# Two heavy down chunks of each pair multiplied as plain float32, and gathered rows copied out by ScalarE alone

## What is computed

```
def swiglu(h, wg, wu, wd):
    return (jax.nn.silu(h @ wg) * (h @ wu)) @ wd

def moe_swiglu(h, w_router, wg, wu, wd):
    ...
    logits = (xt @ w_router).astype(jnp.float32)
    top_v, top_i = lax.top_k(logits, TOP_K)          # TOP_K = 2
    gates = jax.nn.softmax(top_v, axis=-1)
    gate = jnp.sum(jax.nn.one_hot(top_i, N_EXPERTS, dtype=jnp.float32) * gates[..., None], axis=1)
    y = jnp.zeros_like(xt)
    for e in range(N_EXPERTS):
        y = y + gate[:, e:e + 1].astype(xt.dtype) * swiglu(xt, wg[e], wu[e], wd[e])
```

## Time and profile before

| | |
|---|---|
| median of 3 runs | 1589.66 us (1588.79 to 1591.21) |
| the profiled execution | 1587.91 us; span of its instructions 1586.1 us |
| mean granted TensorE clock | 0.986 of full |
| TensorE busy | 1518.3 us, 96% of the span |
| VectorE busy | 1293.6 us, 82% |
| ScalarE busy | 1091.3 us, 69% |
| mixture of experts | from 668 us to the end, 4 pairs |
| DMA | 462.70 MB, 1 MiB for each chunk |

### The profile page before, as it was taken

The page is one execution under the profiler, slowest core; times in us unless marked ns, Lnnn a source line. Parts: engine busy times, 40 slices in busy tenths (PEclk is TensorE's granted clock), DMA queues, the critical chain, the costliest instruction groups (busy, mean ns, idle before and its releaser), DMA issues.

```text
span 1586.1 us, 20833 instructions
## 1 busy us (share of the span) xinstructions
PE 1518.3 (96%) x7379; PEld 1259.1 (79%) x7379; DVE 1293.6 (82%) x1595; ACT 1091.3 (69%) x1435; POOL 117.6 (7%) x242
## 2 busy tenths in 40 slices
PE   6999999999999999699999999999899999999995
PEld 5788788888888888588887788788788787788784
DVE  5686585566545556789999999999999999999998
ACT  3664564645434364278888788888788878788876
POOL 3333431101000010100000000000000000000000
PEclk9999999999999999699999999999999999999998
DMA  9645444535546554369999999999999999999995
GB/s 328 202 157 172 156 158 136 182 115 186 173 146 201 195 179 159 131 240 373 391 398 406 390 378 387 386 407 403 379 387 387 391 409 400 375 387 386 398 409 226
DMA packets 203364, 462.70 MB, mean 292 GB/s; under 512 B 7934, under 2 KB 12428, under 8 KB 203132
## 3 DMA queue, kind: packets, MB, share of 16 engines
q1 hardware_dynamic: 200304, 453.80, 78.3%
q0 software_dynamic: 1904, 5.38, 1.3%
q10 hardware_dynamic: 1052, 2.19, 0.4%
HBM read 460.29 MB, written 1.05 MB: 291 GB/s over the span
## 4 chain that ended last, share of the span: by engine, by line
PE 73%; DVE 11%; DMA 9%; issue 2%; DVEq 2%; ACT 2%; SPq 0%; ACTq 0%
PE ps L2149 8%; PE ps L2151 8%; PE ps L2150 8%; PE ps L2605 7%; PE ps L2607 7%; PE ps L2606 7%; PE ps L2620 6%; DVE wlo_sb L1373 6%; PE ps L2621 6%; DMA raw_sb<-moe_wu 6%; PE ps L2658 2%; DMA raw_sb<-w_in 2%; ACT whi_sb L998 2%; PE ps L2567 1%; DMA raw_sb<-moe_wg 1%
## 5 line engine op out<-in xcount | busy, mean ns | idle before, releaser
L1373 DVE TENSOR_TENSOR wlo_sb<-raw_sb,whi_sb 128x1024 fp32r<-128x1024 f32 x662 | 771.9, 1218 | 37.3 <-ACT whi_sb L998 34.7
L998 ACT ACTIVATE whi_sb<-raw_sb 128x1024 fp32r<-128x1024 f32 x662 | 657.1, 1051 | 153.1 <-PE ps L2607 97.8
L1365 DVE TENSOR_TENSOR wlo_sb<-raw_sb,whi_sb 128x1024 fp32r<-128x1024 f32 (+2 forms) x198 | 230.2, 1204 | 145.6 <-ACT whi_sb L990 144.6
L990 ACT ACTIVATE whi_sb<-raw_sb 128x1024 fp32r<-128x1024 f32 (+2 forms) x198 | 192.3, 1022 | 163.5 <-PE ps L2151 132.1
L2149 PE MATMUL ps<-whi_sb,xlo_sb 128*128 128x512 f32 (+2 forms) x544 | 213.0, 392 | 3.8 <-DVE xlo_sb L1412 3.8
L2151 PE MATMUL ps<-whi_sb,xhi_sb 128*128 128x512 f32 (+2 forms) x544 | 208.7, 384 | 0.0
L2150 PE MATMUL ps<-wlo_sb,xhi_sb 128*128 128x512 f32 (+2 forms) x544 | 208.7, 384 | 0.0
L2605 PE MATMUL ps<-whi_sb,xlo_sb 128*128 128x512 f32 x448 | 181.2, 405 | 4.5 <-DVE wlo_sb L1373 3.8
L2607 PE MATMUL ps<-whi_sb,xhi_sb 128*128 128x512 f32 x448 | 175.4, 392 | 0.0
L2620 PE MATMUL ps<-whi_sb,xhi_sb 128*128 128x512 f32 x448 | 175.1, 391 | 0.0
L2621 PE MATMUL ps<-wlo_sb,xhi_sb 128*128 128x512 f32 x448 | 174.6, 390 | 0.0
(11 more groups left out here) (394 smaller groups left out, 2127.0 us busy)
## 6 DMA issues: line engine op xcount, KB each, us to landing
raw_sb<-moe_wg SPq DMA_DIRECT2D x113, 1024.0 KB, 9.9
raw_sb<-moe_wd SPq DMA_DIRECT2D x112, 1024.0 KB, 10.5
raw_sb<-moe_wu SPq DMA_DIRECT2D x109, 1024.0 KB, 10.6
raw_sb<-w_in SPq DMA_DIRECT2D x40, 1024.0 KB, 5.1
raw_sb<-w_out SPq DMA_DIRECT2D x16, 1024.0 KB, 5.1
raw_sb<-ffn_wg SPq DMA_DIRECT2D x10, 1024.0 KB, 5.1
raw_sb<-ffn_wu SPq DMA_DIRECT2D x10, 1024.0 KB, 5.2
raw_sb<-ffn_wd SPq DMA_DIRECT2D x10, 1024.0 KB, 5.0
```

Of the source, the lines that this page charges most:

```text
L990: nc.scalar.activation(whi[i % SPLIT][:, c:c + k // 2, 0:n], raw[i % RAW][:, c:c + k // 2, 0:n], ACT.Copy).then_inc(hi_ready, 1)
L998: nc.scalar.activation(whi[i % SPLIT][:, c:c + KC // 2, :], moe_raw(i, l)[:, c:c + KC // 2, :], ACT.Copy).then_inc(hi_ready, 1)
L1365: op = V.tensor_tensor(wlo[i % SPLIT][:, c:c + k // 2, 0:n], raw[i % RAW][:, c:c + k // 2, 0:n], whi[i % SPLIT][:, c:c + k // 2, 0:n], ALU ...
L1373: op = V.tensor_tensor(wlo[i % SPLIT][:, c:c + KC // 2, :], moe_raw(i, l)[:, c:c + KC // 2, :], whi[i % SPLIT][:, c:c + KC // 2, :], ALU.s ...
```

## The change

Chunks for which `whole(step)` holds (places 62 and 64 of a pair, 52 and 54 of the first) are no longer split. TensorE multiplies them as plain float32, straight from the raw buffer, with unsplit activations of block 2 in `act_whole` (which lies where that block of `ahi2` lay). ScalarE and VectorE skip them, and the raw buffer is free only once TensorE has read it. VectorE no longer splits block 2 of the heavy activations. Apart from this, all copies of gathered rows go to ScalarE.

```diff
 ROUNDS = 4
+WHOLE_BLOCK = 2
...
+def whole(step):
+    return step.b == HEAVY_JOB and step.chunk.which == "d" and step.chunk.k0 * PART // NC == WHOLE_BLOCK
...
+        plain = ExitStack()
+        sb("below_act_whole", [PART, WHOLE_BLOCK * NC], stack=plain)
+        act_whole = sb("act_whole", [PART, NC], stack=plain)
+        plain.close()
...
+        def is_whole(i, l):
+            return whole((FIRST if first(l) and i < PER else PAIR).steps[i % PER])
...
@@ -704,7 +718,7 @@
             back = i - RAW
             if first(l) and i >= AHEAD[0] and back < AHEAD[0] + len(AHEAD):
                 back -= len(AHEAD)
-            sp.wait_ge(lo_ready, number(AT_MOE, back + 1, PER, l))
+            sp.wait_ge(split_used if back >= 0 and is_whole(back, l) else lo_ready, number(AT_MOE, back + 1, PER, l))
...
@@ -992,11 +1006,17 @@
         def act_hi_moe(act, i, l):
+            if is_whole(i, l):
+                return
             wait_landed_moe(act, i, l)
-            act.wait_ge(split_used, number(AT_MOE, i - SPLIT + 1, PER, l))
+            back = i - SPLIT
+            if back >= 0 and is_whole(back, l):
+                back -= SPLIT
+            act.wait_ge(split_used, number(AT_MOE, back + 1, PER, l))
             for c in range(0, KC, KC // 2):
+                skipped = 2 if c and is_whole(i + 1, l) else 0
                 nc.scalar.activation(whi[i % SPLIT][:, c:c + KC // 2, :], moe_raw(i, l)[:, c:c + KC // 2, :],
-                                     ACT.Copy).then_inc(hi_ready, 1)
+                                     ACT.Copy).then_inc(hi_ready, 1 + skipped)
...
-                nc.scalar.activation(xhi[:, 2 * r:2 * r + 2, a:b],
-                                     xg_tp(n, r)[0].rearrange("p (c n) -> p c n", c=2)[:, :, a:b],
-                                     ACT.Copy).then_inc(xg_hi, 1)
+                hi_ps, lo_ps = (bank.rearrange("p (c n) -> p c n", c=2) for bank in xg_tp(n, r))
+                nc.scalar.activation(xhi[:, 2 * r:2 * r + 2, a:b], hi_ps[:, :, a:b], ACT.Copy).then_inc(xg_hi, 1)
+                if a < PART:
+                    last = nc.scalar.activation(xlo[:, 2 * r:2 * r + 2, 0:PART], lo_ps[:, :, 0:PART], ACT.Copy)
+                if b > PART:
+                    last = nc.scalar.activation(xhi[:, 2 * r:2 * r + 2, PART + LIGHT:2 * PART],
+                                                lo_ps[:, :, PART + LIGHT:2 * PART], ACT.Copy)
+                last.then_inc(xg_lo, 1)
...
-                        nc.scalar.activation(ahi2[:, p * NC:(p + 1) * NC], h_tp(p), ACT.Copy).then_inc(h_hi, 1)
+                        hi = act_whole[:, :] if p == WHOLE_BLOCK else ahi2[:, p * NC:(p + 1) * NC]
+                        nc.scalar.activation(hi, h_tp(p), ACT.Copy).then_inc(h_hi, 1)
...
+            if is_whole(i, l):
+                return
...
-            op.then_inc(lo_ready, 1)
+            skipped = 1 if is_whole(i + 1, l) else 0
+            op.then_inc(lo_ready, 1 + skipped)
...
-            def gathered(n, r):
-                dve.wait_ge(xg_ps, ROUNDS * n + r + 1)
-                src = xg_tp(n, r)[1].rearrange("p (c n) -> p c n", c=2)
-                if not (isinstance(n, int) and n == 1):
-                    last = V.tensor_copy(xlo[:, 2 * r:2 * r + 2, 0:PART], src[:, :, 0:PART])
-                if not first(n):
-                    last = V.tensor_copy(xhi[:, 2 * r:2 * r + 2, PART + LIGHT:2 * PART], src[:, :, PART + LIGHT:2 * PART])
-                last.then_inc(xg_lo, 1)
...
-            gathered(0, 0)
             extras()
-            for r in range(1, ROUNDS):
-                gathered(0, r)
...
-                        V.tensor_tensor(alo2[:, p * NC:(p + 1) * NC], h_tp(p), ahi2[:, p * NC:(p + 1) * NC],
-                                        ALU.subtract).then_inc(h_lo, 1)
+                        if p == WHOLE_BLOCK:
+                            dve.sem_inc(h_lo, 1)
+                        else:
+                            V.tensor_tensor(alo2[:, p * NC:(p + 1) * NC], h_tp(p), ahi2[:, p * NC:(p + 1) * NC],
+                                            ALU.subtract).then_inc(h_lo, 1)
...
-                        if i in LIGHT_GATHER:
-                            gathered(1, LIGHT_GATHER[i])
...
-                    if i in plan.gather:
-                        gathered(j + 2, plan.gather[i])
...
+            def whole_step(i, chunk, j):
+                rows_of, weights = act_whole[:, :], moe_raw(i, j)
+                for c in range(chunk.k):
+                    k = chunk.k0 + c - WHOLE_BLOCK * NC // PART
+                    for h in range(WIDE // NC):
+                        op = mm(acc[:, HEAVY_JOB, h, :], rows_of[:, k * PART:(k + 1) * PART],
+                                weights[:, c * (WIDE // NC) + h, :], start=False, stop=False)
+                op.then_inc(split_used, 1)
...
-                    pe.wait_ge(lo_ready, number(AT_MOE, i + 1, PER, j))
-                    (light_step if b else heavy_step)(i, chunk)
+                    if is_whole(i, j):
+                        wait_landed_moe(pe, i, j)
+                        whole_step(i, chunk, j)
+                    else:
+                        pe.wait_ge(lo_ready, number(AT_MOE, i + 1, PER, j))
+                        (light_step if b else heavy_step)(i, chunk)
```

## The result

The changed kernel takes 1599.41 us (median, 1597.45 to 1600.35), the kernel before, run beside it, 1589.22 us: a ratio of 1.0064, 95% interval 1.0051 to 1.0077, that is 10.2 us slower (8.1 to 12.2). The forecast was 1597.2 us, in the range 1589.5 to 1602.0, and slower.

What follows compares the result with a forecast made beforehand. The prediction took the DMA weight stream as the bound; +8.4 us for late refills, -0.4 at pair starts and -0.5 in the first pair made +7.5, so 1589.66 + 7.5 = 1597.2 us, range 1589.5 to 1602.

Steps and rivals of the forecast that it cites:

- VectorE's 8.3 us are worth nothing: Per pair VectorE sheds 8.3 of 217 us, hidden by the DMA stream; at most 1.2 to 1.4 us elsewhere.
- The rival that VectorE was the bound: VectorE sets the pace, so the change is faster: 1561.6 us if everywhere; chance 8%.
- A plain chunk takes 3.44 us: On TensorE, an unsplit down chunk takes 3.44 us against 2.80 split: +0.64 us, +1.28 a pair.
- The refill waits for TensorE, the queue runs dry: Places 68 and 70: issues 5.8 and 7.5 us later, landings 0.9 and 2.9 us late; 2.8 us a pair.
- 3 x 2.8 = 8.4 us: Loss from holding raw buffers longer at places 68 and 70, summed over pairs 2 to 4: +8.4 us.
- So its 1.28 us are absorbed by the end of the pair: After place 64 TensorE has slack, so its longer chunks cost nothing by the pair's end.
- Given back at two pair starts, -0.4: A fuller queue at the next pair's start wins back a guessed 0.2 us, twice: -0.4 us.
- The first pair, -0.5: First pair escapes the late refill; TensorE's 1.03 us wait for VectorE's copy goes, worth perhaps half: -0.5 us.
- The sum: Whole run: +8.4 for pairs 2 to 4, -0.4 at pair starts, -0.5 in the first pair; total +7.5 us.
- the mechanism forecast: Longer-held raw buffers delay refills and run the DMA queue dry in pairs 2 to 4: 1597.2 us, chance 60%.
- the third rival: TensorE doesn't regain its 1.28 us, so a pair costs 4.2 us: +13.9, 1603.6 us; chance 15%.
- The spread in the prediction: Forecast's own spread, from 2.3 to 3.9 us lost a pair: +5.8 to +10.8 us over the run.

Runs made afterwards that it cites:

- the late refill: Kernel before, every chunk split, but SyncE refills the raw buffers of block 2's two heavy down chunks only once TensorE has multiplied them: 1597.49 us, 1.0043.
- the pair's end reordered: Kernel before with three more multiplications behind each of block 2's two heavy down chunks, and finished rows read and split first: 1588.63 us, 1.0005.
- the reordering there: Changed kernel with finished rows read and split ahead of the chunk three places on, at a job's last down chunk: 1594.65 us, 1.0041.

## Why the prediction was right, and where it was wrong

- **VectorE's 8.3 us are worth nothing:** held. 7 us less busy in a period, and the period 5.5 us longer. The rival that VectorE was the bound is out.
- **A plain chunk takes 3.44 us:** held, 3.44. The Trainium skill (FP8 and Floating Point Precision, "TensorE Precision Notes") has four passes for true float32; with 0.233 us a pass the prediction estimated 3.73 from it. The rule need not be at odds with the measurement, only that price of a pass: an fp32r matmul took 0.43 us at a clock of 0.52, so an estimate of one pass at 1.00 is half of that, 0.215, and sixteen of them make 3.44.
- **The refill waits for TensorE, the queue runs dry:** held, in place, order and flight (5.9 and 4.8 us, 5.2 foreseen). In the changed kernel the issues lie 3.0 and 4.8 us behind the earlier trace rows, less than the 5.8 and 7.5 worked out, because the whole stretch ran some 3 us ahead. The price of 3 x 2.8 = 8.4 us measured 6.8 (4.6 to 8.9) alone. Down chunks issued into a short queue landed after 4.7 to 6.2 us in the runs above (4.7 at place 70 of the fourth pair), where I had taken 5.2. From the fixed 2.0 us of the Trainium skill (DMA: Bandwidth & Descriptors, "Anatomy of one DMA") the estimate was 4.6; the page gives them for the path of transfers that GpSimd issues, SyncE issues these, and none was that fast.
- **"So its 1.28 us are absorbed by the end of the pair": wrong, and the step that failed.** I counted as slack that TensorE does two down chunks in 4.7 us while two land in 5.1. That lets it catch up; it does not make its time free, since it doesn't wait once up to place 82 (53.50 of 53.50 us busy) and what it is late there reaches the next pair's refills. Sized at 0, the term measured 6.0 us alone and 4.0 beside the late refill (10.8 less 6.8); that it fell to +0.8 with the pair's end reordered shows where it is paid, though the landings show only a part of the way. I had read which resource is the bound at place 40 and taken it for the whole pair.
- **"Given back at two pair starts, -0.4": wrong in sign.** Late landings at place 83 hold ScalarE, which holds the finished rows, which hold TensorE; about 3.7 us of the loss went with the reordering there. I had not listed what stands behind ScalarE's wait for a landing.
- **The first pair, -0.5:** right in sign as far as can be told. The copies gave 1.0 us over the run (between 2.4 faster and 0.5 slower), too wide to check 0.5 against.
- **The sum** was +7.5 and came out at 10.2: the mechanism forecast, with the third rival ("two delays add up", +13.9, given 15%) true in good part. That the number came so near is partly luck: the late refill was priced 1.6 us too high and TensorE's longer work 4 to 6 too low. The period shows it, 5.5 us longer where 2.5 to 2.8 were to come. (The spread in the prediction starts at +5.8; by its own terms, 3 x 2.3 - 0.9, it is +6.0.)

## What to carry to other kernels

A stream that is the bound in one stretch of a loop needn't be so in the next: ask TensorE's windows stretch by stretch. Where it is busy without a gap, its added time is carried on, and whether it is paid is settled where the carried lateness meets a short queue: here at the next pair's start, +6.0 us with the old pair's end and +0.8 with the new one. Before a buffer is given a later owner, compare three times: the new release, plus the flight in an empty queue, against the landing of now; moved to where this comes out even, the same change cost nothing that could be measured. And on an in-order engine, put what another engine waits for ahead of what itself may wait for a transfer.

## What the runs showed of the hardware that was not expected

- **The clock falls at short waits.** In the changed kernel TensorE ran at a granted clock of 1.00 (2.4 GHz), waited 2.47 us, and the next eight fp32r matmuls of 512 columns came at 0.43 us with the clock at 0.52 (1.2 GHz): 8 x 0.20 = 1.6 us lost behind the wait itself. The same wait of 1.15 us before left it at 1.00. The length of the wait alone doesn't decide it: in the third pair of the changed kernel one of 1.97 us ended in a fall too, while one of 2.26 us in the run with rows on ScalarE and finished rows first did not.
- **A landing can be late with several transfers under way.** In the changed kernel the issues at 1073.09 and 1076.78 us (places 73 and 74, DMA views below) land at 1083.9 and 1087.2 us, 3.3 apart where down chunks are 2.56 apart, while the engines move 410 GB/s (windows view).

```profile
raw_sb<-moe_wd SPq DMA_DIRECT2D x1, 1024.0 KB, 10.8
...
raw_sb<-moe_wd SPq DMA_DIRECT2D x1, 1024.0 KB, 10.4
```

```profile
1083.90:1087.10 3.20, 1.00 1.03 410
```

  Pairs 2 to 4 have three, two and two such landings outside the dry spells, each 0.7 to 1.3 us late; the kernel before has about one a pair. Two of the seven lie within places 67 to 74 and in their 3.1 us; the other five are part of the difference between that and the period's 5.5. What holds one of sixteen engines back, if it is that, was not tried.
